# Value tiles cut into thirds, gate products moved, and search insertions at other half rounds

## What is computed

```python
def reference_excerpt(h):
    proj = h @ even_w_in                                 # aq ak av ag iq ik iw bq bk bv bg blr
    score = einsum('bth,bths->bts', iw, relu(iq . ik))   # index scores, masked causally
    idx = top_k(score, 256)
    a_out = softmax(aq . ak[idx] + bias) @ av[idx]
    log_a = log_sigmoid(blr @ gate_w2 + gate_b2) / 16    # the low-rank forget gate
    G = cumsum(log_a within a chunk of 64)
    q_dec, k_dec, k_tail = bq * exp(G), bk * exp(-G), bk * exp(G_last - G)
    g_out = tril(q_dec @ k_dec.T) @ bv + q_dec @ S       # S: state before the chunk
    mix = concat(a_out * silu(ag), norm(g_out) * silu(bg)) @ even_w_out
```

## Time and profile before

| | |
|---|---|
| median of 3 runs | 1088.76 us (1088.41 to 1089.56) |
| the profiled execution | 1089.96 us |
| its span in the trace | 1088.2 us |
| TensorE matmuls busy | 1011.9 us, 93% of the span |
| VectorE busy | 696.0 us, 64% |
| ScalarE busy | 458.8 us, 42% |
| GpSimd busy | 272.1 us, 25% |

### The profile page before, as it was taken

How to read it: one execution, slowest core, us unless ns; L and a number is a source line. 1 busy time by engine, 2 the same in 40 slices (tenths; PEclk the granted TensorE clock), 3 DMA queues, 4 the chain that set the end, 5 groups by cost and what they waited for, 6 DMA issues and landing times.

```text
span 1088.2 us, 14635 instructions
## 1 busy us (share of the span) xinstructions
PE 1011.9 (93%) x5642; PEld 817.2 (75%) x5642; DVE 696.0 (64%) x1220; ACT 458.8 (42%) x780; POOL 272.1 (25%) x199
## 2 busy tenths in 40 slices
PE   4997889979999999878999977999999999999997
PEld 3885669968877777656777755888888888888885
DVE  5313679997959779784555464357456767689342
ACT  6323562253423233333454556343426363667131
POOL 1310203101233222311322185311042222206200
PEclk8997999989999999988999988999999999999999
DMA  7251101201022214201101242422231212012152
GB/s 247 64 71 41 40 1 49 70 1 39 29 79 78 68 59 118 62 16 37 33 21 58 97 146 80 153 97 79 76 97 39 58 39 59 20 39 97 58 194 77
DMA packets 71738, 75.81 MB, mean 70 GB/s; under 512 B 5064, under 2 KB 58360, under 8 KB 71672
## 3 DMA queue, kind: packets, MB, share of 16 engines
q1 hardware_dynamic: 70400, 73.30, 21.5%
q10 hardware_dynamic: 1272, 1.62, 1.3%
HBM read 58.13 MB, written 16.25 MB: 68 GB/s over the span
## 4 chain that ended last, share of the span: by engine, by line
PE 82%; DVE 8%; ACT 5%; issue 3%; POOL 1%; DMA 1%; DVEq 0%; SPq 0%; POOLq 0%; ACTq 0%
PE ps L1588 23%; PE ps L1589 22%; PE ps L1590 22%; PE ps L1833 3%; PE ps L1817 2%; PE ps L1676 2%; DVE prob L1371 1%; PE ps L1768 1%; PE ps L1678 1%; PE ps L1765 1%; PE ps L1677 1%; ACT relu L861 1%; PE ps L1736 1%; DVE rank L1334 1%; DVE rank L1333 1%
## 5 line engine op out<-in xcount | busy, mean ns | idle before, releaser
L1588 PE MATMUL ps<-hH,wH 128*128 128x512 f32 x384 | 159.7, 416 | 16.5 <-DVE qkL L1359 10.9
L1229 DVE TENSOR_SCALAR_CACHE_REDUCE junk<-score,cand 128x384 bf16<-128x384 f32 (+2 forms) x192 | 169.7, 943 | 1.3
L1590 PE MATMUL ps<-hH,wL 128*128 128x512 f32 x384 | 152.9, 398 | 0.0
L1589 PE MATMUL ps<-hL,wH 128*128 128x512 f32 x384 | 152.7, 398 | 0.0
L612 POOL TENSOR_TENSOR wL<-raw,wH 128x1024 fp32r<-128x1024 f32 x32 | 77.1, 2413 | 156.8 <-ACT wH L768 156.8
L1588 PEld LDWEIGHTS ps<-hH,wH 128*128 128x128 f32 x384 | 73.9, 192 | 36.5 <-issue 22.4
L1588 PE MATMUL ps<-h1H,w_slot_H 128*128 128x512 f32 x256 | 99.8, 390 | 0.0
L1590 PE MATMUL ps<-h1H,w_slot_L 128*128 128x512 f32 x256 | 99.6, 389 | 0.0
L1589 PE MATMUL ps<-h1L,w_slot_H 128*128 128x512 f32 x256 | 99.6, 389 | 0.0
L1590 PEld LDWEIGHTS ps<-hH,wL 128*128 128x128 f32 x384 | 73.8, 192 | 16.4
L1589 PEld LDWEIGHTS ps<-hL,wH 128*128 128x128 f32 x384 | 74.2, 193 | 13.3
(11 more groups left out here) (242 smaller groups left out, 2259.4 us busy)
## 6 DMA issues: line engine op xcount, KB each, us to landing
raw<-in_even_w_in SPq DMA_DIRECT2D x32, 512.0 KB, 4.0
xt<-in_x SPq DMA_DIRECT2D x16, 512.0 KB, 6.6
raw<-in_odd_w_in SPq DMA_DIRECT2D x16, 512.0 KB, 4.0
gate_d<-gst SPq DMA_DIRECT2D x16, 256.0 KB, 2.2
raw_row<-in_even_w_out SPq DMA_DIRECT2D x8, 512.0 KB, 3.6
x_d<-xt SPq DMA_DIRECT2D x8, 512.0 KB, 2.6
raw_row<-in_odd_w_out SPq DMA_DIRECT2D x8, 512.0 KB, 3.2
xt<-x_d SPq DMA_DIRECT2D x8, 512.0 KB, 4.7
```

What stands on the lines that cost most here:

```text
L1229: return steps(dve.tensor_scalar(junk1[:, j % 3, 0:(qb + 1) * P], score_of(qb), threshold, None, op, ALU.add, accum_out=dst[:, j:j + 1]))
L1588: pe.matmul(dst, lH, rH, start=k == 0, stop=False)
L1589: pe.matmul(dst, lH, rL, start=False, stop=False)
L1590: return pe.matmul(dst, lL, rH, start=False, stop=k == nk - 1)
```

## The change

Five things change.

1. In the index stage TensorE issues a third of a value tile behind each score pair (k 0 to 2, 3 to 5, 6 and 7, that is 9, 9 and 6 matmuls) instead of a whole tile behind every third. ScalarE's order is the same.
2. The four gate products come before the `bv` 1 tiles, into banks 2 to 5, without a wait between them.
3. ScalarE copies all four, and puts Abs, Exp and Ln of both halves one by one behind the copies of the `bv` 1 tiles. The buffers of the gates lie elsewhere. So GpSimd's memsets of `att` and `state` no longer wait for the keys, and ScalarE's first sigmoid of the g stage does.
4. `exponents` stand behind the first and third `bqk` product instead of the second and fourth.
5. VectorE's insertions are at half rounds 20, 25, 28, and the eight steps at 33, 34, 39, 43, 47, 50, 54 and 58.

```diff
-    g_b = at("g_b", [P, T], F32, R2 + 32 * KB)
-    g_b1 = at("g_b1", [P, T], F32, R2 + 36 * KB)
+    g_b = at("g_b", [P, T], F32, R1 + 44 * KB)
+    g_n0 = at("g_n0", [P, T], F32, R1 + 44 * KB)
+    g_n1 = at("g_n1", [P, T], F32, R1 + 40 * KB)
...
-    PRODUCTS += [(name, i, t) for name in ("av", "bv") for i in range(2) for t in range(NT)]
+    PRODUCTS += [(name, i, t) for name, i in (("av", 0), ("av", 1), ("bv", 0)) for t in range(NT)]
     PRODUCTS += [("gate", pr, hf) for pr in range(2) for hf in range(2)]
+    PRODUCTS += [("bv", 1, t) for t in range(NT)]
...
+    GLA_BESIDE = (33, 34, 39, 43, 47, 50, 54, 58)
...
+    def GATE_BANK(pr, hf):
+
+        return 2 + 2 * pr + hf
...
-        pool.wait_ge(proj_full, nth_product("gate", 0, 0))
+        pool.wait_ge(proj_full, nth_product("bqk", BQK_ORDER[0], 0))
...
+        pool.memset(att[:, :, :, :], 0.0).then_inc(gla_const, 1)
+        pool.memset(state[:, 0, :, :], 0.0).then_inc(gla_const, 1)
         for c in range(C_BQK + 2, C_AG + 2):
             low(c)
-        pool.wait_ge(decs_ready, 2)
-        pool.memset(att[:, :, :, :], 0.0).then_inc(gla_const, 1)
-        pool.memset(state[:, 0, :, :], 0.0).then_inc(gla_const, 1)
...
+        for pr, g_l in ((0, g_a), (1, kdec[:, 1, :])):
+            for hf in range(2):
+                act.wait_ge(proj_full, nth_product("gate", pr, hf) + 1)
+                act.activation(g_l[:, hf * HALF:(hf + 1) * HALF], ps[:, GATE_BANK(pr, hf), :], ACT.Identity,
+                               bias=b2[:, pr:pr + 1]).then_inc(proj_copied, 1)
+        act.wait_ge(proj_copied, copy_count("gate", 1, 1))
         for t in range(NT):
             values_out("bv", 1, t)
...
+            if t == 0:
+                own(act.activation(g_n0[:, :], g_a[:, :], ACT.Abs))
+            if t == 1:
+                own(act.activation(g_n1[:, :], kdec[:, 1, :], ACT.Abs))
+            if t == 2:
+                own(act.activation(g_n0[:, :], g_n0[:, :], ACT.Exp, scale=-1.0))
+            if t == 3:
+                own(act.activation(g_n1[:, :], g_n1[:, :], ACT.Exp, scale=-1.0))
+            if t == 4:
+                act.activation(g_n0[:, :], g_n0[:, :], ACT.Ln, bias=onet).then_inc(ln_ready, 1)
+            if t == 5:
+                act.activation(g_n1[:, :], g_n1[:, :], ACT.Ln, bias=onet).then_inc(ln_ready, 1)
...
-            if n % 2:
+            if n % 2 == 0:
                 exponents(n // 2)
...
             if i:
                 act.wait_ge(silu_done, i)
+            else:
+                act.wait_ge(decs_ready, 2)
...
-            if n == 24:
+            if n == 20:
                 dve.wait_ge(gla_const, 1)
                 gates_summed(0)
-            if n == 28:
+            if n == 25:
                 keys_decayed(0)
                 gates_summed(1)
-            if n == 32:
+            if n == 28:
                 keys_decayed(1)
-            for t in range(NT):
-                if n == 34 + 3 * t:
-                    gla_step(t)
+            if n in GLA_BESIDE:
+                gla_step(GLA_BESIDE.index(n))
...
+            if key[0] == "gate":
+                key = PRODUCTS[q - 2 - 4]
...
+        for n in range(len(QBS) * PAIRS):
+            head_scores(QBS[n // PAIRS], n % PAIRS)
+            token_tile("av", 0, n // 3, range(3 * (n % 3), min(3 * (n % 3) + 3, KD)))
+        for t in range(NT):
+            token_tile("av", 1, t)
+        pe.wait_ge(acc_done, len(QBS) * A_HEADS)
+        for t in range(NT):
+            token_tile("bv", 0, t)
         rank_rows = slice(IW_BLR_AT, IW_BLR_AT + RANK)
         pe.wait_ge(w2_in, 64)
         for pr in range(2):
             for hf in range(2):
-                q = nth_product("gate", pr, hf)
-                bank_free(q)
-                pe.matmul(ps[:, q % 2, :], w2[rank_rows, pr, :], iwblr[rank_rows, hf * HALF:(hf + 1) * HALF],
+                pe.matmul(ps[:, GATE_BANK(pr, hf), :], w2[rank_rows, pr, :], iwblr[rank_rows, hf * HALF:(hf + 1) * HALF],
                           start=True, stop=True).then_inc(proj_full, 1)
+        for t in range(NT):
+            token_tile("bv", 1, t)
```

More of the change, by code:

```diff
@@ L887, in _ @@
             high(c)
+        for pr, g_l in ((0, g_a), (1, kdec[:, 1, :])):
[4 more added lines that the diff above has]
+        act.wait_ge(proj_copied, copy_count("gate", 1, 1))
         for t in range(NT):
             values_out("bv", 1, t)
-        for pr, g_l, g_n in ((0, g_a, g_b), (1, kdec[:, 1, :], g_b1)):
-            for hf in range(2):
-                q = nth_product("gate", pr, hf)
[L894 to L899, removed]
+            if t == 0:
[10 more added lines that the diff above has]
+                act.activation(g_n1[:, :], g_n1[:, :], ACT.Ln, bias=onet).then_inc(ln_ready, 1)
         def exponents(pr):
@@ L1244, in gates_summed @@
             dve.wait_ge(ln_ready, pr + 1)
-            g_l, g_n = ((g_a, g_b), (kdec[:, 1, :], g_b1))[pr]
+            g_l, g_n = ((g_a, g_n0), (kdec[:, 1, :], g_n1))[pr]
             own(dve.scalar_tensor_tensor(g_l[:, :], g_l[:, :], 0.0, g_n[:, :], ALU.min, ALU.subtract))
@@ L1612, in column_half, with token_tile @@
             weights_first(q % 2, (wH[:, s], wL[:, s]), hf).then_inc(proj_full, 1)
-        def token_tile(name, i, t):
+        def token_tile(name, i, t, ks=range(KD)):
             c = {"av": C_AV, "bv": C_BV}[name] + 2 * i
             slot, q = dst_slot(c), nth_product(name, i, t)
-            pe.wait_ge(w_lo, c + 2)
-            bank_free(q)
+            if ks[0] == 0:
+                pe.wait_ge(w_lo, c + 2)
+                bank_free(q)
             toks = slice(t * P, (t + 1) * P)
-            for k in range(KD):
+            for k in ks:
                 last = three(ps[:, q % 2, 0:NEAR], (hH[:, k, toks], hL[:, k, toks]),
                              (wH[:, slot:slot + 2, k, :], wL[:, slot:slot + 2, k, :]), k, KD)
-            last.then_inc(proj_full, 1)
+            if ks[-1] == KD - 1:
+                last.then_inc(proj_full, 1)
         pe.wait_ge(w2_in, 48)
```

## The result

The changed kernel takes 1089.93 us in the median of 20 runs (1087.97 to 1094.82), the kernel before 1088.2 in 20 runs beside them (1085.57 to 1091.05). The ratio is 1.0026, with a 95% interval of 1.0014 to 1.0039: 0.1 to 0.4% slower. The forecast was 1079.0 and the range 1066 to 1087.5. The time lies outside the range, and the sign was wrong too.

A forecast was written before the change was run, and what follows sets the result against it. TensorE, with 82% of the chain, was taken to bound the kernel. Gains of 13.9 and 8.3 less 0.5, 8.8, 2.8 and 0.3 gave 9.8 us, so 1079.0; its own range 1073 to 1085, 8 in 10 range 1066 to 1087.5.

The forecast's parts named there:

- Thirds: Index stage: value tiles in thirds fill TensorE's waits for relu and raise its clock; 13.9 us gained, 10.1 to 15.
- Rivals B and C: Index stage: B, thirds gain 4 instead of 13.9, 1088.9, chance 0.16; C, TensorE stays at 1.2 GHz, 1092.8, chance 0.06.
- Gates: Gate products before the last value tiles: 5.5 us of idle time and 2.8 of half speed go; 8.3 gained.
- Step 0: VectorE reaches it at 282.4 us; TensorE wants its att at 283.1, gets it at 283.3 or later; 0.5 lost.
- The waits for bqk copies: VectorE's insertions at half rounds 25 and 28 wait 2.3 and 5.0 us for these copies before step 0.
- the memset of att: GpSimd: memsets move 1.3 us of work in front of weight subtractions that TensorE wants over 10 us later; cost 0.
- Step 1: VectorE's second state update waits 9.7 us for output 0, against 4.4 before, while the search stands still.
- gla_turn(5): TensorE waits for step 4's att, late by counted half rounds and GpSimd meetings; 8.8 us lost, 7.3 to 10.3.
- gla_turn(3) and (4): TensorE's masked scores of these two steps: the forecast had no wait for att and no term here.
- The clock behind the long wait: TensorE's clock falls to 0.50 after the wait near 343 us; 2.8 us lost, lower end 0.
- The join: Second pair product after the search: search ends some 7 us ahead, TensorE alone sets it, all behind it shifts.
- rival D: TensorE waits for VectorE at other step points too, giving 8 us more back; within 2 us of before, chance 0.05.

The follow-up runs named there:

- gates: The changed kernel with whole value tiles and the old half rounds, leaving the gate products' move alone; 1081.74 us, ratio 0.9944 to the kernel before.
- before_slots: The kernel before with eight state buffers instead of four; 1087.91 us, ratio 0.9997 to the kernel before.
- thirds: The kernel before with the index stage's value tiles in thirds and nothing else; 1075.34 us, ratio 0.9890 to the kernel before.
- trim: The changed kernel with GpSimd's subtractions for weight chunks 8 to 23 cut to one of eight parts; 1083.26 us, ratio 0.9977 to the kernel before.
- steps4_7: The changed kernel with steps 4 to 7 at half rounds 44, 47, 51, 55; 1082.61 us, ratio 0.9942 to the kernel before.
- slots: The changed kernel with eight state buffers instead of four, half rounds unchanged; 1073.29 us, ratio 0.9872 to the kernel before.
- step0: The changed kernel with only step 0 moved, to half round 31 from 33; 1082.09 us, ratio 0.9951 to the kernel before.
- oldpos: The changed kernel with all insertions at the old half rounds, keeping thirds and early gates; 1074.00 us, ratio 0.9866 to the kernel before.
- early_slots: The changed kernel with seven of eight steps at other half rounds and eight state buffers; 1070.25 us, ratio 0.9842 to the kernel before.

## Why the prediction was wrong

**Thirds: right in kind, 1.8 too much.** 13.9 was forecast, 12.1 came. The waits for relu went as described. The clock was a smaller and less certain part than its 3.8: two traces with whole tiles, `gates` and `before_slots`, need 74.2 and 74.0 us from the stage's begin to the first `av` 1 copy, where the trace of before needed 75.5 and the changed kernel 63.4. Against those two the gain is 10.9 and 10.7, and that difference is the execution's, not the edit's. Alone the part is worth 13.1 us at the end (`thirds`). Rivals B and C, little gain and a slow clock there, fell: 20 us of the stage ran at 1.00.

**Gates: right.** 8.3 forecast, 8.8 measured, by idle time and half speed as worked out. The prediction has two products ahead of the idle time; the trace has all four there, 3.88 us from 230.35 on, and then 5.46 idle, which leaves the sum as it is. Alone the part gave 6.7 at the end (`gates`); the trace of that kernel has half speed from 208 to 215, which the changed kernel's hasn't.

**Step 0: the step failed.** I put its att at 282.4 and the wait at 0.5; the att came at 288.5 and TensorE, which asked at 285.5, waited 3.7. (By the table TensorE would have asked at 304.69 - 22.2 = 282.5, not at 283.1, which makes the forecast wait 0.6 longer at most.) The search started 10.3 us earlier relative to the stage's begin instead of 12.1, and 1.7 later from the late start. The waits for bqk copies on which I reckoned, 2.3 and 5.0 us, weren't there. In their place stood 9.9 us in which VectorE's short instructions were held, of which the sum had none for this stretch. (1.8 + 1.7 + 9.9 - 7.3 = 6.1, which is the whole delay of step 0's att.) `trim` bears this out: there the holds ahead of step 0 are 0.6 us, the two waits for bqk copies are back with 1.88 and 4.39, the att comes at 285.33 and TensorE waits 1.4. So of the 9.9 us only about 3 made step 0 later; the rest took the place of waiting. VectorE's timeline of the changed kernel, and GpSimd's at the same time:

```profile
176.46 1.08 DVE L1253 TENSOR_SCALAR rej<-cnt 128x6 int32<-128x6 f32 x1
177.57 2.32 DVE L1255 SCALAR_TENSOR_TENSOR cand<-cand,rej 128x6 int32<-128x6 int32 x1
...
225.64 1.24 DVE L1253 TENSOR_SCALAR rej<-cnt 128x6 int32<-128x6 f32 x1
...
237.16 1.40 DVE L1253 TENSOR_SCALAR rej<-cnt 128x6 int32<-128x6 f32 x1
```

```profile
175.10 4.76 POOL L620 TENSOR_TENSOR wL<-raw,wH 128x1024 fp32r<-128x1024 f32 x2 [15.89 <-ACT wH L775]
```

Such an instruction takes 0.17 when nothing is beside it; here it lasts to the end of the subtraction. The earlier trace rows had shown one. I used it only between steps 1 and 4 and left it out where the search starts, although the same weight subtractions run there. In the kernel before VectorE hardly met them: of 170 to 300 us these two are all that last over 0.2.

```profile
230.90 0.70 DVE L1236 TENSOR_SCALAR rej<-cnt 128x6 int32<-128x6 f32 x1
...
288.92 1.54 DVE L1256 COPY small<-g_a 128x16 f32<-128x16 f32 x1 [0.57 <-ACT g_a L905]
```

So a search that starts earlier isn't only shifted; it meets GpSimd at other points. How much it meets is not even fixed for one order: `steps4_7` is the changed kernel up to step 4, and in its trace the holds ahead of step 0 are 4.0 us instead of 9.9. One of the meetings (225.64) is with the memset of att, at 225.65 for 0.95, which the change moved and which I had costed at 0. Behind the wait the clock was 0.50 for some us (288 to 295): 2.3, forecast 0.

**Step 1: right.** Its second state update waits 9.24 us for output 0; 9.7 was forecast. `slots` shows what hangs on it: without it TensorE has no wait at gla_turn(5).

**gla_turn(5): right mechanism, just outside its range.** Forecast 8.8 (7.3 to 10.3), measured 10.7. The terms behind it: from the end of step 1 (312.77) to step 4's att (363.96) are 51.2 us. 13 half rounds and two steps make 45.2 of it, the rest is 6.0 of holds; I took the middle of 0 and 3. `trim` shows the holds as a cause: with most of the subtractions cut, the same stretch takes 45.0 and the wait is 4.0. That TensorE was late itself, by its waits at gla_turn(3) and (4), kept the 10.7 from being longer.

**gla_turn(3) and (4): the step failed.** In the forecast TensorE waits for att at gla_turn(1) and gla_turn(5) alone. It waits 1.12 and 0.90 at the other two as well, 2.2 us in all by the table. The sum has no term for them; VectorE's times had to be carried on to each step, not to step 4 alone.

**The clock behind the long wait: mis-sized.** 2.8 forecast, 5.4 measured. I took the price from one case, an idle time of about 5.5 us with 6 us of work at 0.50 behind it; here the engine worked some 12 us at 0.50 before it had full clock. The longer idle time isn't the reason: behind 4.0 us of waiting in `step0` it was 12 us as well.

**The join: right.** Behind it the stages kept their length. A short spell of half speed near 386 that the trace of before has is missing after; it gives back 1.5 us that I hadn't counted.

The failed terms add up: 1.8 at the thirds, 3.3 and 2.3 at gla_turn(1), 2.2 at (3) and (4), 2.0 at (5), 2.6 for the clock behind it, less 0.5 at the gates and 1.8 at the join; that is 11.9 us too much gain in the forecast of 9.8. With the 1.7 of the late start, the profiled span is 3.8 longer than before. The largest is at gla_turn(1): 5.6 with the half speed behind it. What also went wrong is a chance: rival D has TensorE waiting at other step points too and giving all back. Its time is what was measured, its mechanism a part of it (2.2 us), and I gave it 0.05. The argument stood in the text: the waits of VectorE tie it to TensorE's products, and all of TensorE's later waits hang on that one engine. Errors in VectorE's time therefore don't average out. From step 1 to gla_turn(5) each us that VectorE is late goes into TensorE's wait (`trim`: 6 us fewer holds, 6.7 less waiting), while in `slots` and at the join VectorE's time to spare brought nothing. A range of 7.3 to 10.3 around a middle was for that reason too narrow on its bad side.

## What to carry to other kernels

Work with waits that is inserted at fixed counts into another engine's long loop is tied to that loop's pace, not to its inputs. When inputs come 20 us earlier, reckon for every insertion when its last wait is met and what is queued behind it; an insertion put too early stops the whole loop, and the later ones pay (here step 1, whose 9.2 us came out at step 4). Either leave the counts where they were (here 1074.0 with the gains in front) or deepen the buffer that the early step waits for (1073.3), or do both with new counts (1070.3); and give an ordering error on one engine a one-sided price.

## What the runs showed of the hardware

**Which VectorE instructions are held.** Beside GpSimd's subtraction of 128x1024 (2.4 us each) VectorE's six-element instructions and a plain copy of 16 columns take up to 2.4 us instead of 0.2, while counting passes over up to 1024 columns with an accumulator run at their usual length. The Trainium skill ("Advanced Engine Details and Errata", the section "VectorE Performance Modes") says that GpSimd instructions and Vector instructions with two ports block each other; the trace agrees in that some forms are held and others not. I had not expected it to reach 10 us ahead of step 0 and 6 more up to step 4, nor that moving step 0 by two half rounds would change the second number to 1.1.

**How long half speed lasts.** It doesn't follow from the length of the wait. Behind the 10.7 us the granted clock was 0.50 (1.2 GHz) for 12 us of work and cost 5.4 us. Behind 4.0 us in `step0` and in `trim` it was 0.50 for 12 us of work as well, with TensorE busy nearly all of it (11.89 of 12 us in `step0`). Behind 5.5 us in the kernel before it was 6 us of work. And behind the wait of 3.73 us at gla_turn(1), which the changed kernel and `slots` both have, it was 5 us in the one and under 4 in the other; the row is of `slots`:

```profile
289.00:293.00 4.00, 4.00 (x17) 2.82 (x17) 2.32 (x7) 0.00 (x0) 0.00 (x0) 0.57 0.00 0
```

In `steps4_7`, where TensorE waits 1.1 and 0.9 us at gla_turn(3) and (4), 340 to 380 ran at 1.00. So a price for the clock that is taken from one case can be off by a factor of two either way.

**Half speed without a wait.** While the gate products ran, the clock fell to 0.50 in four of the nine traces that have them early, although TensorE was busy without a gap: in `oldpos`, `steps4_7` and `early_slots` at 199 and for some 7 us, in `gates` at 208. In the other five it stayed at 1.00. It fell during these products in `thirds` (220.5) and `before_slots` (232.1) too, where they stand last. They are eight matmuls of 512 columns and 16 rows, 3.7 us at full clock, between value tiles of 128 rows. At 0.46 us lost of each, 7 us at half speed cost about 3, an estimate. The four executions took 0.8 to 4.5 us more than the medians of their kernels. That the products cause the fall isn't shown, since no run was made to test it.

**Do the parts add?** `thirds` and `gates` gave 13.1 and 6.7, both together 14.4 with the old insertions and 16.3 with moved ones and eight state buffers (`early_slots`). Neither is clear of 19.7 by its interval; the loss of all of it with the new half rounds is. Once TensorE is early, VectorE's order decides how much of it stays. Whether half rounds exist that would give the full 19.7 was not tried.
